# Eight experts on one core: samples in fixed slots, prompt tokens in 120, the gate applied as Y is evicted, Y scattered in a high and a low part

## The chip, the cores and the metric

The kernel runs on one core of one Trainium2 chip. The metric is the device time of that core in microseconds (us), as the median of several runs. The profile is of one execution on the same core.

## What is computed

One step of a two-layer trunk (SSD and RG-LRU mixers, a dense SwiGLU in layer 0, two of eight experts in layer 1) for 256 prompt tokens and 8 sample tokens, width 1024. The change touches the experts alone:

```python
def swiglu(x, wg, wu, wd):
    return (jax.nn.silu(x @ wg) * (x @ wu)) @ wd

def moe_swiglu(x, w_r, wg, wu, wd):
    logits = (x @ w_r).astype(jnp.float32)
    top_v, top_i = lax.top_k(logits, TOP_K)            # TOP_K = 2
    gates = jax.nn.softmax(top_v, axis=-1)
    dense_gate = jnp.sum(jax.nn.one_hot(top_i, N_EXPERTS, dtype=jnp.float32) * gates[..., None], axis=-2)
    out = jnp.zeros_like(x)
    for e in range(N_EXPERTS):                         # 8 experts, inner width 3584
        out = out + dense_gate[..., e:e + 1].astype(x.dtype) * swiglu(x, wg[e], wu[e], wd[e])
    return out
```

Everything is float32. After it comes a last RMSNorm of the prompt rows and the sample rows.

## The kernel before

The engines run programs of their own, written out in the order in which they issue, and meet by semaphores. The experts' part is a loop of **jobs**, one per expert (if an expert gets more tokens than it has slots, all eight are run again in a second and third pass, up to 24 jobs; `passes` decides it).

**Weights.** An expert's weights come as 42 units of 128x2048 floats (1 MB each), in the order of `STREAM`: step s = 0 to 6 takes two units of gate, two of up, and two of down for the step before (6 units in a full step). SP loads them into a ring of 6 slots (L631). ScalarE (ACT) rounds a unit to `w_hi` (fp32r), VectorE (DVE) subtracts it into `w_lo` (also fp32r); three slots of each. A product is three fp32r matmuls in TensorE (PE): `hi*hi`, `lo*hi`, `hi*lo` (`product`), so a unit is 12 matmuls of 128x512 and an expert 504. ACT may round unit p only when PE has used up unit p-3, and DVE follows ACT: this chain of PE, ACT, DVE and PE again (`split` on both engines) comes round once in three units.

**Tokens.** `sel_m` says which token lies in which of the 128 slots of the expert. `gather` turns it into the expert's input, XG transposed, by full fp32 matmuls: 8 blocks of 128 columns, for each the three token tiles (128, 128 and 8 rows). ACT and DVE evict it as `xg_hi` and `xg_lo`. It is made one job ahead: at the end of job j, between `transposes(6)` and `down(6)`, for job j+1. Right behind it three transposes bring the gated selection `sel_g` into S_BANK, which DVE copies to `sct`.

**Results.** Y of a job (two banks, 128 slots x 1024) is copied to `ysb` by ACT (`ysb`, 2 ACTIVATEs in the last iteration of its job loop). In the next job, after `down` of steps 0 to 5, `scatter(p)` makes one full fp32 matmul `sct` by `ysb` each, for token tile p//2 and column half p%2; two of the six have only the 8 sample rows. DVE adds the result to `acc` (`add_back`). After the last job six scatters follow through one bank, each waiting for the add before it; then ACT and DVE normalise the three tiles and POOL stores them.

In the profile a full fp32 matmul stands as two MATMUL records, an fp32r matmul and a transpose (`flip`, L806) as one; L802 is `mm`. L1211 is ACT's `f`, L1506 DVE's `tt`, L1503 its `stt`. `hntok`, `acc`, `ysb`, `sel_m`, `sel_g` and, before the change, `sct` all lie in `moe_arena` and bear its name.

## Time and profile before

| | us |
|---|---|
| median of 3 runs | 1937.28 |
| lowest, highest | 1935.87, 1945.31 |
| span of the profiled execution | 1943.8 |
| experts' products, first to last (850.15 to 1917.6) | 1067 |

The three runs are 1935.87, 1945.31 and 1937.28 us; of the profiled execution only its span is given, 1943.8 us from the first instruction to the last. PE is busy for 95% of that span, DVE for 71%, ACT for 55%, and the mean granted clock is 0.963 of full speed. A row of the timeline gives an instruction's start, its time, its operands and the idle time before it with what ended it. Successive matmuls overlap in it, so what one of them costs is the distance from its start to the next one's start, not its own time.

### The profile page before, as it was taken

What the parts mean: (1) busy time and instruction counts of PE and PEld (TensorE: products, weight loads), DVE (VectorE), ACT (ScalarE), POOL (GpSimd) and SP (SyncE); (2) the same over time, 40 slices, a digit from 0 to 9 for tenths busy, and PEclk for the clock granted to TensorE, in tenths of its full rate; (3) what the DMA queues carried; (4) which work ended last, traced back from release to release, by engine and by line L of the source; (5) the groups of instructions that cost most, each with busy time, mean ns of one, the idle gap of its engine ahead of it and who ended that gap; (6) DMA issues with size and microseconds to landing.
All of it is one profiled execution on the core that took longest, in us unless ns stands there. A gap on an engine that the chain in (4) does not pass through costs nothing.

```text
span 1943.8 us, 24842 instructions
## 1 busy us (share of the span) xinstructions
PE 1845.3 (95%) x9284; PEld 1513.6 (78%) x9284; DVE 1371.4 (71%) x1458; ACT 1075.4 (55%) x1101; POOL 167.2 (9%) x175
## 2 busy tenths in 40 slices
PE   7989889999999988889999999999999999999996
PEld 5867778999886677868778778787787787787873
DVE  4655865554465487458879788788788787887883
ACT  2236444443222654346667577676676775776772
POOL 2014530000100453000000000000000000000000
PEclk9999889999999988879999999999999999999997
DMA  8424434555643443339979899799799798997980
GB/s 246 136 89 150 140 112 145 181 151 168 193 130 100 136 135 121 119 136 365 351 285 360 296 346 358 271 369 360 277 365 352 279 365 284 358 355 284 364 321 24
DMA packets 257030, 465.48 MB, mean 239 GB/s; under 512 B 8492, under 2 KB 108196, under 8 KB 256928
## 3 DMA queue, kind: packets, MB, share of 16 engines
q1 hardware_dynamic: 249384, 441.84, 65.6%
q0 software_dynamic: 6384, 21.28, 3.7%
q10 hardware_dynamic: 1192, 1.44, 0.3%
q8 instruction: 43, 0.70, 0.2%
q14 instruction: 27, 0.22, 0.0%
HBM read 453.70 MB, written 11.15 MB: 239 GB/s over the span
## 4 chain that ended last, share of the span: by engine, by line
PE 86%; DVE 8%; ACT 3%; issue 2%; ACTq 0%; DMA 0%; POOL 0%; DVEq 0%; POOLq 0%
PE bank L802 83%; DVE arena L1503 3%; PE bank L806 2%; DVE arena L1506 1%; ACT w_hi L1211 1%; ACT arena L1211 1%; DVE w_lo L1506 1%; DVE fw_lo L1506 1%; DMA arena<-in_state_lru_conv 0%; DVE rs L1506 0%; DVE rs L1760 0%; ACTq L592 0%; ACT L1211 0%; ACT moe_arena L1211 0%; DVE rs L1535 0%
## 5 line engine op out<-in xcount | busy, mean ns | idle before, releaser
L1506 DVE TENSOR_TENSOR w_lo<-wring,w_hi 128x2048 fp32r<-128x2048 f32 x336 | 768.3, 2290 | 128.9 <-ACT w_hi L1211 127.1
L1211 ACT ACTIVATE w_hi<-wring 128x2048 fp32r<-128x2048 f32 x336 | 643.7, 1919 | 248.7 <-PE bank L802 248.5
L802 PE MATMUL bank<-w_hi,xg_hi 128*128 128x512 f32 x896 | 370.9, 414 | 3.0 <-DVE xg_lo L1506 1.6
L802 PE MATMUL bank<-w_lo,xg_hi 128*128 128x512 f32 x896 | 351.0, 392 | 0.0
L802 PE MATMUL bank<-w_hi,xg_lo 128*128 128x512 f32 x896 | 349.9, 390 | 0.0
L802 PE MATMUL bank<-hn,wring 128*128 128x264 f32 x1152 | 273.1, 398 | 6.1 <-DVE hn L1503 6.1
L802 PEld LDWEIGHTS bank<-hn,wring 128*128 128x128 f32 x1152 | 223.1, 196 | 50.8 <-issue 9.8
L802 PEld LDWEIGHTS bank<-w_hi,xg_hi 128*128 128x128 f32 x896 | 168.9, 189 | 55.6 <-issue 16.5
L802 PEld LDWEIGHTS bank<-w_hi,xg_lo 128*128 128x128 f32 x896 | 169.3, 189 | 39.9 <-issue 7.7
L802 PEld LDWEIGHTS bank<-w_lo,xg_hi 128*128 128x128 f32 x896 | 168.7, 188 | 36.9
L1506 DVE TENSOR_TENSOR fw_lo<-wring,fw_hi 128x2048 fp32r<-128x2048 f32 (+1 forms) x54 | 115.2, 2134 | 109.7 <-ACT fw_hi L1211 109.7
L802 PE MATMUL bank<-w_hi,at_hi 128*128 128x512 f32 x448 | 175.1, 391 | 0.0
L802 PE MATMUL bank<-w_hi,at_lo 128*128 128x512 f32 x448 | 174.4, 389 | 0.0
L802 PE MATMUL bank<-w_lo,at_hi 128*128 128x512 f32 x448 | 174.3, 389 | 0.0
L1211 ACT ACTIVATE arena<-bank 128x264 f32<-128x264 f32 (+3 forms) x100 | 43.1, 444 | 218.5 <-PE bank L802 207.6
L802 PE MATMUL bank<-moe_arena 128*128 128x128 f32 (+2 forms) x540 | 142.4, 387 | 11.4 <-DVE moe_arena L1863 6.2
L1211 ACT ACTIVATE fw_hi<-wring 128x2048 fp32r<-128x2048 f32 (+1 forms) x54 | 94.8, 1756 | 89.8 <-PE bank L802 89.8
L802 PEld LDWEIGHTS bank<-moe_arena 128*128 128x128 f32 (+1 forms) x540 | 79.1, 194 | 45.2 <-issue 17.0
L802 PEld LDWEIGHTS bank<-w_lo,at_hi 128*128 128x128 f32 x448 | 84.1, 188 | 17.6
L802 PEld LDWEIGHTS bank<-w_hi,at_hi 128*128 128x128 f32 x448 | 84.1, 188 | 17.4
L802 PEld LDWEIGHTS bank<-w_hi,at_lo 128*128 128x128 f32 x448 | 84.1, 188 | 17.2
L773 POOL DMA_DIRECT2D out<-moe_arena x2 | 1.1, 534 | 1117.5 <-DVE moe_arena L1503 1117.5
(215 smaller groups left out, 2329.9 us busy)
## 6 DMA issues: line engine op xcount, KB each, us to landing
wring<-in_moe_w_gate SPq DMA_DIRECT2D x112, 1024.0 KB, 5.2
wring<-in_moe_w_up SPq DMA_DIRECT2D x112, 1024.0 KB, 5.3
wring<-in_moe_w_down SPq DMA_DIRECT2D x112, 1024.0 KB, 5.1
wring<-in_w_in SPq DMA_DIRECT2D x36, 1024.0 KB, 5.2
wring<-in_w_out SPq DMA_DIRECT2D x16, 1024.0 KB, 5.1
wring<-in_ffn_w_gate SPq DMA_DIRECT2D x11, 1024.0 KB, 5.3
wring<-in_ffn_w_up SPq DMA_DIRECT2D x11, 1024.0 KB, 5.4
wring<-in_ffn_w_down SPq DMA_DIRECT2D x16, 704.0 KB, 4.6
```

The lines of the kernel that those rows point to most:

```text
L773: pool.dma_start(o[0][0, t * P:(t + 1) * P, :], outt[:, t, :]).then_inc(y_out, 16)
L802: return nc.tensor.matmul(out, lhsT, rhs, start=start, stop=stop)
L806: return nc.tensor.transpose(out, in_, ident[0:k, 0:k])
L1211: return nc.scalar.activation(out, in_, fn, **kw)
L1503: return V.scalar_tensor_tensor(out=out, in0=in0, scalar=scalar, in1=in1, op0=op0, op1=op1)
L1506: return V.tensor_tensor(out, in0, in1, op)
```

## The change

SLOTS becomes 120. Slots 120 to 127 of every expert hold the eight samples: they are written into `xg_hi` and `xg_lo` once, before the first job, and the gather fills the other 120 columns from two token tiles, not three. A sample that did not choose an expert has gate 0 there. Token tile 2 is now tokens 136 to 263, of which only rows 120 to 127 count.

The gate no longer sits in the scatter matrix. `slots_back(j)` in step 5 transposes `sel_m` of the job at hand (two transposes) and makes `gslot`, the gate of each slot, with three matmuls of one column; DVE copies both out and only then chooses for the next job (`choose`, so far in step 2's iteration). At the end of a job ACT evicts Y times `gslot` as `ysb_hi` (fp32r), and DVE (`results`) makes `ysb_lo` and adds the sample rows straight into `acc`. There are four scatters a job, each as two fp32r matmuls (`ysb_hi`, `ysb_lo`) with `sct` as the stationary side. After the last job the four scatters go to four banks. The output tiles are normalised in the order 2, 0, 1.

```diff
-SLOTS = P
-SCATTERS = 7
+SLOTS = P - NB
+S_FILLS = 5
...
+        TOK0 = (0, P, T - P)
+        ROWS = (slice(0, P), slice(0, P), slice(96, P))
...
+        TAIL_BANKS = (BA, BB, BN, Q0)
...
-                    ins = mm(out[0:n, t * NE:(t + 1) * NE], hn[:, k, t * P:t * P + n], w_router[:, k, :],
+                    ins = mm(out[:, t * NE:(t + 1) * NE], hn[:, k, TOK0[t]:TOK0[t] + P], w_router[:, k, :],
...
-            for t in range(4):
-                terms = [(ones, i) for i in range(min(t, 3))] + ([(before, t)] if t < 3 else [])
+            for t in range(3):
+                terms = [(ones, i) for i in range(t)] + ([(before, t)] if t < 2 else [])
...
-                        for t in range(3):
-                            n = P if t < 2 else NB
-                            ins = mm(out[:, q * P:(q + 1) * P], hntok[0:n, t, d0:d0 + P], sel_m[0:n, t, :],
-                                     start=t == 0, stop=t == 2)
+                        for t in range(2):
+                            ins = mm(out[:, q * P:(q + 1) * P], hntok[:, t, d0:d0 + P], sel_m[:, t, :],
+                                     start=t == 0, stop=t == 1)
...
-            def scatter(p, n, last_adds=0):
+            def scatter(out, p):
 
                 t, h = p // 2, p % 2
-                rows = P if t < 2 else NB
-                if last_adds:
-                    pe.wait_ge(acc_done, last_adds)
-                else:
-                    pe.wait_ge(evac[S_BANK], moe0[S_BANK] + n)
-                mm(bank[S_BANK][0:rows, :], sct[:, t, 0:rows], ysb[:, 512 * h:512 * h + 512]
-                   ).then_inc(full[S_BANK], 1)
+                for i, y in enumerate((ysb_hi, ysb_lo)):
+                    ins = mm(out[:, :], sct[:, t, :], y[:, 512 * h:512 * h + 512], start=i == 0, stop=i == 1)
+                return ins
+
+            def slots_back(j):
+
+                pe.wait_ge(evac[S_BANK], moe0[S_BANK] + S_FILLS * j + 4)
+                out = bank[S_BANK]
+                for t in range(2):
+                    flip(out[:, t * P:(t + 1) * P], sel_m[:, t, :])
+                for t in range(3):
+                    ins = mm(out[:, 2 * P:2 * P + 1], sel_m[:, t, :] if t < 2 else ident[:, :], cur[:, 2, t:t + 1],
+                             start=t == 0, stop=t == 2)
+                ins.then_inc(full[S_BANK], 1)
...
-                        pe.wait_ge(ysb_ready, 2 * j + 1)
+                        pe.wait_ge(y_free, j + 1)
                     if s > 0:
                         down(s - 1, j, STREAM.index(("d", s - 1, 0)), n - 1)
-                        scatter(s - 1, j * SCATTERS + s - 1)
+                    if 0 < s < 5:
+                        pe.wait_ge(evac[S_BANK], moe0[S_BANK] + S_FILLS * j + s - 1)
+                        scatter(bank[S_BANK], s - 1).then_inc(full[S_BANK], 1)
+                    if s == 5:
+                        slots_back(j)
...
-                pe.wait_ge(selg_ready, j + 1)
-                pe.wait_ge(evac[S_BANK], moe0[S_BANK] + j * SCATTERS + 6)
-                for t in range(3):
-                    n = P if t < 2 else NB
-                    ins = flip(bank[S_BANK][:, t * P:t * P + n], sel_g[0:n, t, :])
-                ins.then_inc(full[S_BANK], 1)
...
-            pe.wait_ge(ysb_ready, 2 * jobs + 1)
-            for p in range(6):
-                scatter(p, jobs * SCATTERS + p, last_adds=p)
+            pe.wait_ge(y_free, jobs + 1)
+            for p in range(4):
+                scatter(bank[TAIL_BANKS[p]], p).then_inc(tail_full, 1)
...
+            xs = hn[:, :, TP:T]
+            f(xg_hi.rearrange("p i (q s) -> p (i q) s", s=P)[:, :, SLOTS:P], xs).then_inc(xs_ready, 1)
...
+                        act.wait_ge(evac[S_BANK], moe0[S_BANK] + (j + 1) * S_FILLS)
                         for h in range(2):
-                            f(ysb[:, 512 * h:512 * h + 512], bank[Y_BANKS[h]][:, :]).then_inc(ysb_ready, 1)
+                            f(ysb_hi[:, 512 * h:512 * h + 512], bank[Y_BANKS[h]][:, :], scale=gslot[:, :]
+                              ).then_inc(ysb_ready, 1)
...
+                V.tensor_copy(gate_of[:, js, 0:2].rearrange("p e t -> p t e"), gates[:, 0:2, :])
+                if p == 0:
+                    V.tensor_copy(gate_of[:, js, 2:3].rearrange("p e t -> p t e"), gates[:, 2:3, :])
+                else:
+                    V.memset(gate_of[:, js, 2:3], 0.0)
+            V.memset(sel_m[:, :, :], 0.0)
+            V.memset(sct[:, :, :].bitcast(F32), 0.0).then_inc(sct_zero, 1)
...
-                for t in range(3):
-                    ins = V.tensor_scalar(sel_m[:, t, :], iota[:, :], cur[:, 0, t:t + 1], cur[:, 1, t:t + 1],
-                                          ALU.is_equal, ALU.mult)
+                for t in range(2):
+                    ins = V.tensor_scalar(sel_m[:, t, 0:SLOTS], iota[:, 0:SLOTS], cur[:, 0, t:t + 1],
+                                          cur[:, 1, t:t + 1], ALU.is_equal, ALU.mult)
                 ins.then_inc(selm_ready, 1)
 
-            def gated(j):
-                dve.wait_ge(selm_ready, j + 1)
-                for t in range(3):
-                    ins = V.tensor_scalar(sel_g[:, t, :], sel_m[:, t, :], cur[:, 2, t:t + 1], None, ALU.mult)
-                ins.then_inc(selg_ready, 1)
-
             choose(0)
-            gated(0)
             for p in range(1, SPLITS):
                 split(0, p)
...
-                evacd(tt(xg_lo[:, i], filled("gather", i)[:, :], xg_hi[:, i].bitcast(F32), ALU.subtract), "gather", i)
-
-            def add_back(p, n):
+                evacd(low_slots(i, filled("gather", i)), "gather", i)
+
+            def add_back(out, p):
                 t, h = p // 2, p % 2
-                rows = P if t < 2 else NB
-                dve.wait_ge(full[S_BANK], moe0[S_BANK] + n + 1)
-                v = acc[0:rows, t, 512 * h:512 * h + 512]
-                return tt(v, v, bank[S_BANK][0:rows, :], ALU.add)
+                v = acc[:, t, 512 * h:512 * h + 512]
+                return tt(v, v, out[:, :], ALU.add)
+
+            def results(j):
+
+                for h in range(2):
+                    dve.wait_ge(ysb_ready, 2 * j + h + 1)
+                    hs = slice(512 * h, 512 * h + 512)
+                    stt(ysb_lo[:, hs], bank[Y_BANKS[h]][:, :], gslot[:, :], ysb_hi[:, hs].bitcast(F32), ALU.mult,
+                        ALU.subtract)
+                    v = acc[ROWS[2], 2, hs]
+                    ins = stt(v, bank[Y_BANKS[h]][ROWS[2], :], gslot[ROWS[2], :], v, ALU.mult, ALU.add)
+                ins.then_inc(y_free, 1)
...
-                    if (mat, h) == ("d", 1) and s < STEPS - 1:
-                        add_back(s, j * SCATTERS + s).then_inc(evac[S_BANK], 1)
-                    if (mat, s, h) == ("d", 2, 1):
+                    if (mat, h) == ("d", 1) and s < 5:
+                        dve.wait_ge(full[S_BANK], moe0[S_BANK] + j * S_FILLS + s + 1)
+                        if s < 4:
+                            add_back(bank[S_BANK], s).then_inc(evac[S_BANK], 1)
+                    if (mat, s, h) == ("d", 4, 1):
+                        V.tensor_copy(gslot[:, :], bank[S_BANK][:, 2 * P:2 * P + 1])
+                        V.tensor_copy(sct[:, :, :], bank[S_BANK][:, 0:2 * P].rearrange("p (t n) -> p t n", t=2)
+                                      ).then_inc(evac[S_BANK], 1)
+                        dve.wait_ge(evac[S_BANK], moe0[S_BANK] + (j + 1) * S_FILLS)
                         choose(j + 1)
                     if (mat, s, h) == ("d", STEPS - 2, 1):
                         low_part(STEPS - 1, n + 1)
                         for i, b in enumerate(X_BANKS):
                             dve.wait_ge(xg_hi_ready, 2 * j + 2 + i + 1)
-                            tt(xg_lo[:, i], bank[b][:, :], xg_hi[:, i].bitcast(F32), ALU.subtract
-                               ).then_inc(evac[b], 1)
-                        dve.wait_ge(full[S_BANK], moe0[S_BANK] + j * SCATTERS + 7)
-                        V.tensor_copy(sct[:, 0:2, :], bank[S_BANK][:, 0:2 * P].rearrange("p (t n) -> p t n", t=2))
-                        V.tensor_copy(sct[:, 2, 0:NB], bank[S_BANK][:, 2 * P:2 * P + NB]).then_inc(evac[S_BANK], 1)
-                        gated(j + 1)
+                            low_slots(i, bank[b]).then_inc(evac[b], 1)
+                    if p == PER_JOB + SPLITS - 1:
+                        results(j)
...
+            V.memset(ysb_hi[:, :].bitcast(F32), 0.0)
+            V.memset(ysb_lo[:, :].bitcast(F32), 0.0).then_inc(y_free, 1)
...
-            for p in range(6):
-                add_back(p, jobs * SCATTERS + p).then_inc(acc_done, 1)
+            for p in range(4):
+                dve.wait_ge(tail_full, p + 1)
+                add_back(bank[TAIL_BANKS[p]], p).then_inc(acc_done, 1)
 
             dve.wait_ge(gfin_landed, 16)
-            for t in range(3):
-                n = P if t < 2 else NB
-                dve.wait_ge(act_step, 2 * t + 2)
-                link(V.reciprocal(ssum[0:n, t:t + 1], ssum[0:n, t:t + 1]))
-                stt(outt[0:n, t, :], acc[0:n, t, :], ssum[0:n, t:t + 1], gfin[0:n, :], ALU.mult, ALU.mult
-                    ).then_inc(y_ready, 1)
+            for i, t in enumerate((2, 0, 1)):
+                r = ROWS[t]
+                dve.wait_ge(act_step, 2 * i + 2)
+                link(V.reciprocal(ssum[r, t:t + 1], ssum[r, t:t + 1]))
+                stt(outt[r, t, :], acc[r, t, :], ssum[r, t:t + 1], gfin[r, :], ALU.mult, ALU.mult).then_inc(y_ready, 1)
```

PE around step 5 of a job, before: down(4), a scatter of the sample rows, and the next step's gate product.

```order
L802 MATMUL bank<-w_hi,at_hi 128x512
L802 MATMUL bank<-w_hi,at_lo 128x512
L802 MATMUL bank<-w_lo,at_hi 128x512
L802 MATMUL bank<-moe_arena 8x512
L1106 REGISTER_ALU
L1108 REGISTER_ALU
L802 MATMUL bank<-w_hi,xg_hi 128x512
```

The same place now (L810 is `mm`, L814 is `flip`):

```order
L810 MATMUL bank<-w_lo,at_hi 128x512
L1152 REGISTER_ALU
L814 MATMUL bank<-ident,moe_arena 128x128 x2
L810 MATMUL bank<-moe_arena 128x1 x2
L810 MATMUL bank<-moe_arena,ident 128x1
L1113 REGISTER_ALU
L1115 REGISTER_ALU
L810 MATMUL bank<-w_hi,xg_hi 128x512
```

The scatter is gone there, and `slots_back` has come in.

PE at the end of a job, before, between down(5) and down(6):

```order
L802 MATMUL bank<-moe_arena 8x512
L1116 REGISTER_ALU
L806 MATMUL bank<-ident,moe_arena 128x128 x4
L1164 REGISTER_ALU
L802 MATMUL bank<-moe_arena 128x128 x24
L1173 REGISTER_ALU
L806 MATMUL bank<-ident,moe_arena 128x128 x2
L806 MATMUL bank<-ident,moe_arena 128x8
```

And now:

```order
L810 MATMUL bank<-w_lo,at_hi 128x512
L1123 REGISTER_ALU
L814 MATMUL bank<-ident,moe_arena 128x128 x4
L1182 REGISTER_ALU
L810 MATMUL bank<-moe_arena 128x128 x16
L1130 REGISTER_ALU
L1133 REGISTER_ALU
L810 MATMUL bank<-w_hi,at_hi 128x512
```

The scatter before the transposes, 8 of the 24 gather matmuls and the three transposes behind them are gone.

DVE at the end of a job, before, from the evictions of the gathered input to the first three units of the next job:

```order
L1506 TENSOR_TENSOR xg_lo<-bank,xg_hi 128x512
L1917 REGISTER_ALU
L1918 COPY moe_arena<-bank 128x256
L1919 COPY moe_arena<-bank 128x8
L1870 TENSOR_SCALAR moe_arena<-moe_arena 128x128 x3
L1798 REGISTER_ALU
L1506 TENSOR_TENSOR w_lo<-wring,w_hi 128x2048
L1798 REGISTER_ALU
L1506 TENSOR_TENSOR w_lo<-wring,w_hi 128x2048
L1798 REGISTER_ALU
L1506 TENSOR_TENSOR w_lo<-wring,w_hi 128x2048
```

And now:

```order
L1523 TENSOR_TENSOR xg_lo<-bank,xg_hi 128x4x120
L1815 REGISTER_ALU
L1523 TENSOR_TENSOR w_lo<-wring,w_hi 128x2048
L1815 REGISTER_ALU
L1523 TENSOR_TENSOR w_lo<-wring,w_hi 128x2048
L1907 REGISTER_ALU
L1520 SCALAR_TENSOR_TENSOR ysb_lo<-bank,moe_arena,ysb_hi 128x512
L1520 SCALAR_TENSOR_TENSOR moe_arena<-bank,moe_arena 32x512
...
L1815 REGISTER_ALU
L1523 TENSOR_TENSOR w_lo<-wring,w_hi 128x2048
```

The small copies ahead of unit 0 are gone; `results` (four instructions, two of them left out above) stands between unit 1 and unit 2.

## Rows read from the trace of the kernel before

**Rows 1.** The page: busy time of each engine and share of the span.

```profile
PE 1845.3 (95%) x9284; PEld 1513.6 (78%) x9284; DVE 1371.4 (71%) x1458; ACT 1075.4 (55%) x1101; POOL 167.2 (9%) x175
```

**Rows 2.** Busy time by stretch: PE, PEld, DVE, ACT, POOL, clock, DMA share, GB/s.

```profile
1110.00:1245.00 135.00, 134.81 (x607) 106.85 (x606) 111.02 (x76) 92.02 (x62) 0.00 (x0) 1.00 0.92 326
```

**Rows 3.** Waits of PE from 1000 to 1800 us: total, times, longest.

```profile
PE bank L802 <- DVE w_lo L1506: 1.1, 5, 0.2
```

**Rows 4.** Timeline of PE, a 128-row scatter among products: start, us, instruction.

```profile
1280.51 0.39 PE L802 MATMUL bank<-w_lo,at_hi 128*128 128x512 f32 x1
1280.74 1.02 PE L802 MATMUL bank<-moe_arena 128*128 128x512 f32 x2
...
1281.82 0.39 PE L802 MATMUL bank<-w_hi,xg_lo 128*128 128x512 f32 x1
```

**Rows 5.** Timeline of PE, an 8-row scatter among products.

```profile
1218.09 0.39 PE L802 MATMUL bank<-w_lo,at_hi 128*128 128x512 f32 x1
...
1219.70 0.39 PE L802 MATMUL bank<-w_hi,xg_lo 128*128 128x512 f32 x1
...
1224.71 0.39 PE L802 MATMUL bank<-w_lo,xg_hi 128*128 128x512 f32 x1
```

**Rows 6.** Timeline of PE, gather and transposes at the end of a job.

```profile
1237.82 8.41 PE L802 MATMUL bank<-moe_arena 128*128 128x128 f32 x48
1246.16 0.59 PE L806 MATMUL bank<-ident,moe_arena 128*128 128x128 f32 x3
...
1247.02 0.39 PE L802 MATMUL bank<-w_hi,at_lo 128*128 128x512 f32 x1
```

**Rows 7.** Timeline of PEld (weight loads), matmuls of 8 columns in `rank`.

```profile
826.43 0.75 PEld L802 LDWEIGHTS bank<-moe_arena,ones 128*128 128x128 f32 x6
```

**Rows 8.** Timelines at a job's end: ACT's eviction of Y, DVE's splits, PE.

```profile
1252.46 1.09 ACT L1211 ACTIVATE moe_arena<-bank 128x512 f32<-128x512 f32 x2 [0.75 <-PE bank L802]
1253.43 1.92 ACT L1211 ACTIVATE w_hi<-wring 128x2048 fp32r<-128x2048 f32 x1
...
1251.74 2.29 DVE L1506 TENSOR_TENSOR w_lo<-wring,w_hi 128x2048 fp32r<-128x2048 f32 x1 [0.74 <-ACT w_hi L1211]
1255.38 2.29 DVE L1506 TENSOR_TENSOR w_lo<-wring,w_hi 128x2048 fp32r<-128x2048 f32 x1 [1.35 <-ACT w_hi L1211]
...
1260.95 0.50 PE L802 MATMUL bank<-w_hi,xg_hi 128*128 128x512 f32 x1 [0.22 <-DVE w_lo L1506]
```

**Rows 9.** The router's logits: timeline of PE, then its count in a stretch.

```profile
810.74 7.45 PE L802 MATMUL bank<-w_router,hn 128*128 128x8 f32 x48 [5.81 <-issue]
...
817.50:818.00 0.50, 0.50 (x16) 0.50 0.00 0
```

**Rows 10.** Router to first expert: timelines of PE and DVE, a stretch as rows 2.

```profile
833.50 15.03 PE L802 MATMUL bank<-moe_arena 128*128 128x128 f32 x48 [6.23 <-DVE moe_arena L1863]
...
830.69 0.91 DVE L1852 MEMSET moe_arena<- 128x1024 f32 x1 [0.15 <-issue]
...
850.00:856.00 6.00, 5.85 (x14) 4.59 (x15) 0.00 (x0) 0.24 (x1) 0.00 (x0) 0.50 0.00 0
```

**Rows 11.** The end: four steps of the chain of waits, then ACT's timeline.

```profile
1917.85 1.09 ACT moe_arena L1211 x2
...
1928.78 0.70 DVE moe_arena L1506
...
1936.25 1.29 DVE moe_arena L1503
...
1939.22 0.49 POOL out L775
...
1923.80 1.06 ACT L1211 ACTIVATE moe_arena<-moe_arena 128x1024 f32<-128x1024 f32 x1 [4.86 <-DVE moe_arena L1506]
...
1926.26 0.29 ACT L1211 ACTIVATE moe_arena<-moe_arena,eps 128x1 f32<-128x1 f32 x1
```

**Rows 12.** Busy time by stretch, columns as in rows 2, where the ring refills.

```profile
864.00:879.00 15.00, 15.00 (x69) 12.18 (x68) 13.61 (x8) 11.44 (x9) 0.00 (x0) 1.00 1.03 384
```

More of the change, by code:

```diff
@@ L413, in trunk @@
         cur = carve(3, 3)
-        sel_m = carve(3, P)
-        sel_g = carve(3, P)
-        sct = carve(3, P)
+        sel_m = carve(2, P)
+        gslot = carve(1)
         m1 = carve(3)
         gsum = carve(3)
-        outt = hntok
         gfin = carve(D)
```

79 lines of the change are left out of this document (44 added, 35 removed).

## The prediction

> **What bounds the kernel now.** I read the page first: PE is busy for 95% of the span, DVE for 71%, ACT for 55% [rows 1]. Then the busy time by stretch, for one expert out of the loop: PE is busy in all but 0.2 of 135 us, at full clock, DVE in 111, ACT in 92, and the weight stream brings 326 GB/s [rows 2]. Then PE's waits: from 1000 to 1800 us it stood still for 1.1 us in all, for DVE's `w_lo` [rows 3]. So in the experts PE's own instructions set the time, and whatever PE no longer does is won, as long as the weight splits and the stream keep up. Since matmuls overlap, I price each by the distance between starts. An fp32r product costs 0.228 us (22 distances in 1219.70 to 1224.71) [rows 5]; an expert's 42 units of 12 products make 115 us. The eight jobs take 1067 us from first to last product (table of times), 133 each, so some 18 us go to scatters, gather and transposes. The change works on these.
>
> **Scatters, per job.** From the product before a 128-row scatter to the second product behind it are 1.31 us, of which two are product distances: 0.86 us for the scatter [rows 4]. With 8 rows it is 1.61 - 0.46 = 1.15 us [rows 5]; fewer rows made it no cheaper. Before: 4 x 0.86 + 2 x 1.15 = 5.7 us. After: 4 x 2 fp32r matmuls of the shape of the products, 8 x 0.228 = 1.8 us. No row shows `sct` by `ysb_hi`, but its shape and type are those of rows 5; dearer than 0.35 each (a start and a stop in one bank) I would not expect. Gain 3.9 us, lower end 2.9.
>
> **Gather, per job.** 48 records in 8.34 us are 0.174 each [rows 6]. A third of them goes: 2.8 us. The evictions of 480 instead of 512 columns change nothing that counts.
>
> **`slots_back` for the three transposes, per job.** The transposes took 1246.16 to 1247.02 less one product, 0.63 us [rows 6]. Now there are two (0.42) and three fp32 matmuls of one column, six records. The nearest rows are `rank`'s with 8 columns, 0.125 a record [rows 7]: 0.75. Below it lies 0.04, the narrow router records [rows 9], above it the gather's 0.174. I take 1.15, net +0.5 us a job; ends 0.0 and +0.8.
>
> Together 3.9 + 2.8 - 0.5 = 6.2 us a job, eight jobs, the last one too: **-49.6 us**.
>
> **The new wait at the end of a job.** ACT may round unit 2 of the next job only when PE is through with down(6), and evicts Y first: at 1252.46, then unit 2 at 1253.43; DVE splits it from 1255.38 to 1257.67 [rows 8]. PE needs it 2 x 12 products after down(6), at 1257.7. It is just in time, and unit 3 is already 0.2 us late at 1260.95 [rows 8]. Now `results` stands on DVE between units 1 and 2: four instructions that wait for ACT's eviction. Behind them wait DVE's splits of units 2 and 3, and PE for them. DVE ends unit 1 at 1254.0 on that scale (1251.74 + 2.29). Since it no longer has the small copies to do and PE starts down(6) 0.5 us sooner, I reckon from the start S of down(6) (1246.68, where the gap behind the transposes of rows 6 ends): unit 1 done at S+7.3; `results` four times 0.6 (a 128x512 add takes 0.70 and overlaps by 0.1 [rows 11]) to S+9.7; unit 2 until S+12.0. PE needs it at S+11.05: 0.95 us late. Unit 3 was late before, by 0.5 us from start to start (12 products after 1257.7 would be 1260.45), and is now in time because PE comes later. Net **+0.45 us**, seven times: **+3.2**. Ends: 0 (if the four overlap more) and +1.5 (if each takes 0.85 and unit 3 is late too).
>
> **Other moves on DVE.** `choose` moves to step 4's iteration, where it takes the place of an add (0.6), with a copy and a cast of some 0.5. The copies and `sel_g` behind the gather and two 8-row adds are gone. DVE's sum stays near 111 us of now 127. The splits have about 0.8 us to spare a round of three units: PE frees a slot, ACT starts 0.4 us later, takes 1.92, DVE 2.29 [rows 8], against 3 x 2.72 us of PE. I cost it at nothing; the scatters that shrink were no part of that slack, they only lengthened it.
>
> **Head.** Router to first expert: token tile 2 is now 128 wide in the logits. Of 48 records the last 16 were narrow, at 0.04, the others 0.21 ((817.5 - 810.74) / 32) [rows 9]: +2.7 us. Eight transposes of `hntok` go, at 0.17 (0.52 / 3 [rows 6]): -1.4. On DVE the 0.91 us memset moves out of the way [rows 10] and small ones come and go. The first gather ran at half clock, 15.03 us [rows 10]; a third is 5.0. Sum **-4.6**, ends -2 and -7. The first products then run at half clock, 14 records in 6 us [rows 10], and the gain in starting sooner may shorten or lengthen this by 1.5 us.
>
> **Tail.** From ACT's eviction at 1917.85 to the last store's issue at 1939.22 are 21.4 us: six scatters in turn, each behind the add before [rows 11]. Now: eviction 0.6, `results` until 3.4, four pairs at half clock (0.43 a record) end at 7.1, adds (0.70) run beside. ACT's first norm starts at 5.2 behind the first add and takes 2.75 (1923.80 to 1926.55, with its table load), two more at 1.45: 10.9; DVE's last multiply 1.45 more: 12.3 [rows 11]. Saved 9.0, less 0.7 since the last store is now a 128-row tile: **-8.3**, ends -6 and -10.
>
> **Sum.** -49.6 + 3.2 - 4.6 - 8.3 = -59.3 us: the profiled span of 1943.8 becomes 1884.5. The profiled execution lies 6.5 us above the median of the runs, 1937.28; the same difference taken from that median gives **1878 us**.
>
> **A rule against it: the weight stream.** The stream brought 384 GB/s over 15 us when the ring refilled [rows 12] and has to bring 44.04 MB in 127 us, 347 on average, and 6.29 MB in 17.3 us within a step of 17.3 us (72 products, transposes, one scatter), 364. So the rows leave room. The Trainium skill, in DMA: Bandwidth & Descriptors, section Where 436 GB/s comes from, has transfers from HBM to SBUF bound at about 358 GB/s per core. By that a step's six loads take 17.6 us, more than PE's 17.3; but over a whole expert it would be 123 us, below the 127 of PE, and the ring's six slots even it out, so the sum would be the same. The trace goes above that figure, for 15 us at least.
>
> **Rivals.**
> 1. *The splits become the bound at the job's end.* `results` costs more than 0.6 an instruction, or its delay runs on through units 3 to 5. For it: unit 3 is late already [rows 8]. Against it: each later unit wins back 0.4 us on DVE. At 2.5 us a job: 7 x 2 more, 1892. Chance 0.10.
> 2. *The clock falls at the job's border.* PE idled 6.2 us before the first gather, and that gather and the first products ran at half clock [rows 10]; a wait of nearly 1 us now comes seven times. Against it: it is far shorter, and the waits of 0.2 us so far left the clock at 1.00 [rows 2, 8]. At half clock 14 records take 6 us instead of 3.2 [rows 10]: 7 x 2.8 = 20 more, 1898. Chance 0.06.
> 3. *The stream holds at what it shows for a whole expert, 326 GB/s* [rows 2]. Then a job stays at 133 us and only head and tail are won: 1924. Against it [rows 12]. Chance 0.03.
> 4. *Slower: a second pass.* If one expert gets over 120 prompt tokens (so far: over 128 tokens with the samples), `passes` becomes 24: sixteen more jobs of 127 us, 3910 us. The mean is 256 x 2 / 8 = 64. The reference's router on its own drawn inputs gives the fullest expert 96 prompt tokens, so it decides only for other inputs. Chance 0.01.
> 5. *The fp32r scatter is no cheaper than the fp32 one* (a pair at 0.86): 4 x 0.4 x 8 = 13 less won, 1891. Chance 0.05.
>
> **How the numbers follow.** My case has 0.75. Its open ends: scatters +8, `slots_back` -4 to +3, the wait -3 to +7, head and tail -4 to +5; not all at once, -13 to +15. With rivals 1, 2 and 5 inside, the range is 1864 to 1899. A measurement of this kernel tells about 0.5% (10 us) from no change; faster by more than that holds in all cases but rival 4 and something unseen: faster 0.96, same 0.02, slower 0.02.
>
> **What would show it.** In the profile after: two records of `ysb_hi` and `ysb_lo` at 0.23 us start to start; a gather of 32 records in 5.6 us; a job of 127 us from gather to gather; PE waiting for `w_lo` once a job by 0.7 to 1.0 us at unit 2, right behind four SCALAR_TENSOR_TENSOR on DVE; the clock at 1.00 throughout the loop; 340 to 350 GB/s. I am wrong if the job takes over 129 us, or if PE's waits in the loop exceed 2 us a job.

## The result, and the profile after

The changed kernel takes 1889.62 us (median of 4 runs, 1887.01 to 1891.59), the kernel before 1937.01 beside it: a ratio of 0.974, 95% interval 0.972 to 0.976. Its profiled execution spans 1887.7 us, 56.1 less than before. That is more than the 47.4 us between the medians, because the profiled execution before was a long one: its span of 1943.8 us exceeds the whole time of the other three runs before (1935.87, 1936.75 and 1937.28 us). The page, busy time of each engine:

```profile
PE 1782.1 (94%) x9128; PEld 1490.4 (79%) x9128; DVE 1377.5 (73%) x1438; ACT 1076.2 (57%) x1102; POOL 167.1 (9%) x175
```

PE still sets the time; it is busy for 63 us less than in [rows 1]. One whole job, from gather to gather, as in [rows 2] (us, then PE, PEld, DVE, ACT, POOL, clock, DMA share, GB/s):

```profile
1103.00:1231.60 128.60, 127.32 (x581) 103.21 (x580) 111.95 (x74) 92.20 (x63) 0.00 (x0) 1.00 0.96 342
```

DVE and ACT do about the same work as before in 4.6 us less, the clock is full, and the stream brings 342 GB/s; before it was 326 in the window of [rows 2], and 331 from gather to gather. PE, which was busy for all but 0.2 us, now stands still for 1.3. From start of gather to start of gather the job takes 128.56 us (1088.21, 1216.77), before it took 133.20 (1104.63, 1237.82). The span's loss splits into four parts (the jobs are eight times 4.64, and the first products what is left between them and the head):

| us | forecast | measured |
|---|---|---|
| start to first product of the experts | -4.6 | -8.8 |
| first products at full instead of half clock | 0 | -2.9 |
| eight jobs | -46.4 | -37.1 |
| tail | -8.3 | -7.2 |
| sum | -59.3 | -56.0 |

The timeline of PE, a scatter among products (start, us, instruction), against [rows 4, 5]:

```profile
1127.38 0.39 PE L810 MATMUL bank<-ysb_hi,sct 128*128 128x512 f32 x1
1127.61 0.39 PE L810 MATMUL bank<-ysb_lo,sct 128*128 128x512 f32 x1
1127.84 0.40 PE L810 MATMUL bank<-w_hi,xg_hi 128*128 128x512 f32 x1
```

The pair costs 0.46 us from start to start, where one fp32 matmul cost 0.86. `slots_back`, and the gather against [rows 6]:

```profile
1198.20 0.38 PE L814 MATMUL bank<-ident,moe_arena 128*128 128x128 f32 x2
1198.42 0.50 PE L810 MATMUL bank<-moe_arena 128*128 128x1 f32 x4
1198.78 0.36 PE L810 MATMUL bank<-moe_arena,ident 128*128 128x1 f32 x2
1199.01 0.48 PE L810 MATMUL bank<-w_hi,xg_hi 128*128 128x512 f32 x1
...
1216.77 3.74 PE L810 MATMUL bank<-moe_arena 128*128 128x128 f32 x32
1220.26 0.48 PE L810 MATMUL bank<-w_hi,at_hi 128*128 128x512 f32 x1
```

32 records go by in 3.49 us, 0.109 each; before they were 0.174 each. `slots_back` takes 0.81 us. The place of the new wait, DVE and PE:

```profile
1225.34 2.29 DVE L1523 TENSOR_TENSOR w_lo<-wring,w_hi 128x2048 fp32r<-128x2048 f32 x1
1227.55 0.75 DVE L1520 SCALAR_TENSOR_TENSOR ysb_lo<-bank,moe_arena,ysb_hi 128x512 fp32r<-128x512 f32 x1
1228.31 0.76 DVE L1520 SCALAR_TENSOR_TENSOR moe_arena<-bank,moe_arena 32x512 f32<-32x512 f32 x1
...
1230.64 2.29 DVE L1523 TENSOR_TENSOR w_lo<-wring,w_hi 128x2048 fp32r<-128x2048 f32 x1
...
1231.31 0.40 PE L810 MATMUL bank<-w_lo,xg_hi 128*128 128x512 f32 x1
1232.98 0.50 PE L810 MATMUL bank<-w_hi,xg_hi 128*128 128x512 f32 x1 [1.28 <-DVE w_lo L1523]
```

Each of the four `results` instructions takes 0.77 us, unit 2 is split by 1232.93, and PE gets it 1.67 us after the product before it, 1.44 more than a product distance. PE's waits from 1000 to 1800 us (total, times, longest), against [rows 3]:

```profile
PE bank L810 <- DVE w_lo L1523: 7.7, 6, 1.3
```

And this, which the forecast has no step for: two products of one stretch, 40 product distances apart, nothing but products between; first now, then such a stretch of before.

```profile
1117.11 0.40 PE L810 MATMUL bank<-w_hi,xg_lo 128*128 128x512 f32 x1
...
1126.45 0.40 PE L810 MATMUL bank<-w_lo,at_hi 128*128 128x512 f32 x1
```

```profile
1137.57 0.40 PE L802 MATMUL bank<-w_hi,xg_lo 128*128 128x512 f32 x1
...
1146.65 0.39 PE L802 MATMUL bank<-w_lo,at_hi 128*128 128x512 f32 x1
```

The 9.34 us by 40 are 0.2335 us a product, at full clock and with no wait; 22 of before took 0.228 each [rows 5], and these 40 of before took 9.08, 0.227. Times 504 products this is worth 3 us a job. Most of the experiments are about it.

Head: the first gather and the first product of the experts, against [rows 10].

```profile
834.22 5.62 PE L810 MATMUL bank<-moe_arena 128*128 128x128 f32 x32 [6.01 <-DVE moe_arena L1884]
841.38 0.49 PE L810 MATMUL bank<-w_hi,xg_hi 128*128 128x512 f32 x1 [1.54 <-DVE xg_lo L1523]
841.71 0.40 PE L810 MATMUL bank<-w_hi,xg_lo 128*128 128x512 f32 x1
```

Busy time by stretch during this gather (columns as above):

```profile
836.00:838.00 2.00, 2.00 (x12) 2.00 (x11) 2.00 (x2) 0.00 (x0) 0.00 (x0) 0.50 0.40 31
838.00:840.00 2.00, 1.84 (x16) 1.65 (x15) 1.02 (x2) 0.69 (x2) 0.00 (x0) 1.00 0.95 358
```

The clock rose from 0.50 to 1.00 about two thirds through the gather, so that the products behind it are 0.23 to 0.33 us apart and not 0.43. Before, it rose only at 856 us, 22 us after the gather's start. Tail: ACT's eviction, the first scatter matmul, the four adds, the last store, against [rows 11].

```profile
1868.94 1.26 ACT L1223 ACTIVATE ysb_hi<-bank,moe_arena 128x512 fp32r<-128x512 f32 x2 [5.08 <-PE bank L810]
...
1872.78 0.80 PE L810 MATMUL bank<-ysb_hi,sct 128*128 128x512 f32 x1 [3.92 <-DVE moe_arena L1520]
...
1874.33 2.70 DVE L1523 TENSOR_TENSOR moe_arena<-moe_arena,bank 128x512 f32<-128x512 f32 x4 [1.61 <-PE bank L810]
...
1882.58 0.54 POOL L781 DMA_DIRECT2D out<-moe_arena  x1 [0.85 <-DVE moe_arena L1520]
```

From eviction to the last store's issue are 13.6 us, before 21.4. The forecast had 12.3 and 0.7 more behind the issue. Of the 1.3 us between them 0.4 lies ahead of the first scatter (3.84 us after the eviction began, not 3.4), which is `results` again, 0.5 between it and the first add (1.55 us, not 1.1), and 0.4 between ACT's last norm step and the store's issue.

The tail before is not the same in every execution. Its second scatter, in the chain of waits of the kernel before and then of a kernel of experiment 3 (offsets 256; 1024), which differs from it only in places in SBUF:

```profile
1920.96 2.09 PE bank L802 x2
```

```profile
1919.30 1.14 PE bank L806 x2
```

In the first the clock had fallen to 0.50 at 1920.9 us, in the second it stayed at 1.00 until 1929.1. From the last product's start to the end of the span the first takes 26.5 us and the second 21.9. The kernels of experiments 2, 3 and 5 leave this tail's program as it was, and they show the same two lengths: 21.9 us four times and 26.4 or 26.5 twice. The changed kernel's is 19.3. So 4.5 of the 7.2 us won in the tail hang on the execution that was profiled before.

### The profile page after: what moved, and what is told of

It is laid out like the page before. It is cut to its first block, busy times and chain, and to the rows that moved or that the text cites. A ratio compares the mean times of both kernels' runs of the same rounds, so it can differ in the third digit from the quotient of the medians.

```text
span 1887.7 us, 24534 instructions
## 1 busy us (share of the span) xinstructions
PE 1782.1 (94%) x9128; PEld 1490.4 (79%) x9128; DVE 1377.5 (73%) x1438; ACT 1076.2 (57%) x1102; POOL 167.1 (9%) x175
## 3 DMA queue, kind: packets, MB, share of 16 engines
q10 hardware_dynamic: 1192, 1.44, 0.3%
## 4 chain that ended last, share of the span: by engine, by line
PE 85%; DVE 9%; ACT 3%; issue 2%; ACTq 1%; DMA 0%; POOL 0%; DVEq 0%; POOLq 0%
PE bank L810 83%; DVE arena L1520 3%; PE bank L814 2%; ACT arena L1223 1%; DVE arena L1523 1%; DVE w_lo L1523 1%; DVE moe_arena L1520 1%; DVE fw_lo L1523 1%; DMA arena<-in_state_lru_conv 0%; ACT L1223 0%; DVE rs L1523 0%; DVE rs L1777 0%; ACTq L600 0%; ACT ysb_hi L1223 0%; DVE rs L1552 0%
## 5 line engine op out<-in xcount | busy, mean ns | idle before, releaser
L810 PE MATMUL bank<-w_hi,xg_hi 128*128 128x512 f32 x896 | 359.0, 401 | 10.6 <-DVE w_lo L1523 9.0
L810 PE MATMUL bank<-w_lo,xg_hi 128*128 128x512 f32 x896 | 354.5, 396 | 0.0
L810 PE MATMUL bank<-w_hi,xg_lo 128*128 128x512 f32 x896 | 354.4, 396 | 0.0
L810 PE MATMUL bank<-hn,wring 128*128 128x264 f32 x1152 | 272.5, 397 | 6.2 <-DVE hn L1520 6.1
L810 PEld LDWEIGHTS bank<-hn,wring 128*128 128x128 f32 x1152 | 222.7, 196 | 50.6 <-issue 9.8
L810 PEld LDWEIGHTS bank<-w_hi,xg_hi 128*128 128x128 f32 x896 | 168.4, 188 | 52.6 <-DVE w_lo L1523 12.6
L810 PEld LDWEIGHTS bank<-w_lo,xg_hi 128*128 128x128 f32 x896 | 168.2, 188 | 40.3
L810 PEld LDWEIGHTS bank<-w_hi,xg_lo 128*128 128x128 f32 x896 | 168.4, 188 | 38.2
L810 PE MATMUL bank<-w_hi,at_lo 128*128 128x512 f32 x448 | 177.7, 397 | 0.0
L810 PE MATMUL bank<-w_hi,at_hi 128*128 128x512 f32 x448 | 177.1, 395 | 0.0
L810 PE MATMUL bank<-w_lo,at_hi 128*128 128x512 f32 x448 | 176.6, 394 | 0.0
L810 PEld LDWEIGHTS bank<-w_hi,at_hi 128*128 128x128 f32 x448 | 84.1, 188 | 20.7
L810 PEld LDWEIGHTS bank<-w_lo,at_hi 128*128 128x128 f32 x448 | 84.1, 188 | 20.0
L810 PEld LDWEIGHTS bank<-w_hi,at_lo 128*128 128x128 f32 x448 | 84.1, 188 | 19.8
L810 PE MATMUL bank<-hn_hi,fw_hi 128*128 128x264 f32 x352 | 88.9, 288 | 4.4 <-ACT hn_hi L1223 4.4
L810 PE MATMUL bank<-hn_hi,fw_lo 128*128 128x264 f32 x352 | 88.8, 287 | 0.0
```

Source lines behind the costliest of these rows:

```text
L810: return nc.tensor.matmul(out, lhsT, rhs, start=start, stop=stop)
```

## The experiments

**What can make the same product dearer?** The change moves buffers. `sct` now stands ahead of `w_hi`, and paddings went in, so the operands of a product lie elsewhere in SBUF. (In `product`, `xg` or `at` is the stationary operand, 128x128, and w the moving one, 128x512.) In bytes of a partition, modulo 256: before, `w_hi`, `w_lo`, `xg_hi`, `xg_lo`, `at_hi` and `at_lo` all are at 128; now `w_hi` and `w_lo` are at 0 and the other four at 160. Theory A: it is where the stationary operand itself lies. Theory G, formed when A fell: it is the distance between the stationary operand (xg, at) and the moving one (w). The expectations of experiment 4 have these two names the other way round. The rival of both is that the order of the changed program, or its fuller stream, slows PE. (Where an expectation names a further theory by a letter, it says there what that theory holds.)

**1. The stationary operands back to where they were modulo 256.** `xg` and `at` at 128, w left at 0.

```diff
-        sb("to_hn", [P, 552])
+        sb("to_hn", [P, 544])
...
         xg_hi, xg_lo = (sb(n, [P, 2, 4 * P], F32R) for n in ("xg_hi", "xg_lo"))
+        sb("to_ysb", [P, 32])
```

> The changed kernel with one difference: the stationary operands at_hi, at_lo, xg_hi, xg_lo start 32 bytes lower in SBUF, on a multiple of 128 bytes as they did before the change (in the changed kernel they start 32 bytes past one); ysb_hi and ysb_lo move up by 96 bytes. Same instructions, same order. Theory A, placement: the distance between products, 0.2332 us in the changed kernel against 0.2267 before, comes from where the stationary operands lie. Then it goes back to 0.2267, 504 products a job win 3.3 us, 8 jobs 26 us: about 1863 us, with PE's wait for w_lo at unit 2 somewhat longer (1.6 to 1.8 us). Theory B, company: the distance grew because DVE and the weight stream have less time per product now. Then it stays at 0.233 and the time at 1889.

Measured: 1885.16 us (1880.93 to 1886.12), ratio to before 0.9729 (0.9713 to 0.9745). Theory A wanted 1863 us; this is 4 us under the changed kernel. Forty product distances took 9.34 us (1115.47 to 1124.81), as in the changed kernel, and a job 128.27 us, 0.3 less. A falls: the stationary operand's own place is not enough.

**2. The kernel before, with its stationary operands shifted by 32 bytes.**

```diff
         w_hi, w_lo = (sb(n, [P, SPLITS, UNIT], F32R) for n in ("w_hi", "w_lo"))
+        sb("shift", [P, 8])
```

> The kernel before with one difference: a gap of 32 bytes ahead of xg_hi, so that xg_hi, xg_lo, at_hi, at_lo start 32 bytes past a multiple of 128. Theory A, placement: the products come at 0.2332 instead of 0.2267 us, 4032 of them cost 26 us more: about 1963 us. Theory B, company: nothing changes, 1937 us.

Measured: 1956.82 us (1956.7 to 1962.45), ratio 1.0116 (1.0099 to 1.0133), 20 us slower by nothing but a gap, where 26 were expected. Forty product distances of this kernel:

```profile
1138.13 0.39 PE L803 MATMUL bank<-w_hi,xg_lo 128*128 128x512 f32 x1
...
1147.46 0.40 PE L803 MATMUL bank<-w_lo,at_hi 128*128 128x512 f32 x1
```

Here 40 take 9.33 us, 0.233 each: the dear product stands in the old program, with the old stream. So neither the new order nor the stream makes it. The job takes 135.65 us, 2.45 more than before.

**3. All six buffers shifted by 32 bytes, and other distances.** In the kernel before. First, the gap ahead of `w_hi`, so that everything moves together:

```diff
+        sb("shift", [P, 8])
         w_hi, w_lo = (sb(n, [P, SPLITS, UNIT], F32R) for n in ("w_hi", "w_lo"))
```

> The kernel before, all of w_hi, w_lo, xg_hi, xg_lo, at_hi, at_lo 32 bytes further. Relative places are as before, absolute ones are not a multiple of 64. Theory G, relative place: 0.2267, 1937 us. Theory H, absolute place: 0.233, 1957 us, as where the stationary operands alone were shifted.

Then gaps in front of single buffers. With `xg_hi` 0, `xg_lo` 128 and `at` 2048 bytes past a multiple of 4096 from w:

```diff
+        sb("to_xg_lo", [P, 32])
         xg_lo = sb("xg_lo", [P, 2, 4 * P], F32R)
+        sb("to_at_hi", [P, 480])
```

> The kernel before, only the places of the stationary operands differ. Measured from the moving operand w_hi modulo 4096 bytes (where all four lay at 0 before): xg_hi 0, xg_lo 128, at_hi 2048, at_lo 2048. Read from the trace: the distance between products of each kind. Theory G, relative place: a product takes 0.2267 us only where the stationary operand lies at 0 from the moving one (modulo some power of two up to 4096). Then the products next to xg_lo go to 0.233 and those with at_hi and at_lo tell whether the power is above 2048. Theory H, absolute place of w: the changed kernel is slower because w_hi starts at a multiple of 256 there and not here; then all stay at 0.2267 here, and only shifts that are no multiple of 64 cost. Time 1937 to 1960 us.

With `xg` 256 and `at` 1024 bytes past it (gaps of 64 and 192 floats):

> As the run before, with xg_hi and xg_lo at 256 and at_hi and at_lo at 1024 from w_hi modulo 4096. Theory G: 0.233 where 256 or 1024 is not a multiple of the period, 0.2267 where it is. Theory H: 0.2267 for all. Time 1937 to 1960 us.

With `xg_hi` 64, `xg_lo` 192 and `at` 256 (gaps of 16, 32 and 16 floats):

> The kernel before with xg_hi 64 bytes and xg_lo 192 bytes past a multiple of 256 from w_hi and w_lo, and at_hi and at_lo a multiple of 256 from them as before. So far 0, 256, 1024 and 2048 gave 0.2267 us between products, and 32, 128 and 160 gave 0.233. Theory G1 (a multiple of 256 bytes is wanted): both 64 and 192 are slow, the 336 gate and up products of a job at 0.233, those of down at 0.2267: 336 x 8 x 0.0065 = 17 us more than the kernel before, 1954 us. Theory G2 (the period is 64 and 128 was slow for another reason): all fast, 1937. Between them: one of the two slow, 1942 to 1950, and then the products beside xg_lo and those beside xg_hi alone differ.

Measured, each beside before on its own chip, with the time of 40 product distances of a stretch like those above, a job from gather to gather, and the mean distance, from 1000 to 1750 us, behind each kind of product (the three kernels in the middle were run once each):

| | us | before | 40 distances | job | hi by `xg_hi` | hi by `xg_lo` | lo by `xg_hi` | hi by `at_hi` |
|---|---|---|---|---|---|---|---|---|
| before | | | 9.08 | 133.20 | 0.229 | 0.227 | 0.229 | 0.227 |
| only xg, at by 32 | 1956.8 | 1936.6 | 9.33 | 135.65 | 0.233 | 0.233 | 0.233 | 0.233 |
| all by 32 | 1940.0 | 1939.3 | 9.09 | 133.33 | 0.228 | 0.228 | 0.229 | 0.227 |
| 0, 128; 2048 | 1946.5 | 1939.3 | 9.15 | 134.00 | 0.232 | 0.234 | 0.228 | 0.227 |
| 256; 1024 | 1939.6 | 1939.3 | 9.09 | 133.20 | 0.228 | 0.227 | 0.229 | 0.227 |
| 64, 192; 256 | 1952.0 | 1944.7 | 9.21 | 134.38 | 0.229 | 0.235 | 0.231 | 0.229 |

The jobs say more than the times: the tail told of above (26.4 or 26.5 us against 21.9) adds 4.5 us to an execution, as it did in the one of 1946.5. Shifting all six costs 0.1 us a job at most: what counts is the relation. The offsets 0, 256, 1024 and 2048 bytes are cheap, 32 and 128 dear. (The 128-column tiles inside `xg` and `at` themselves lie 512 bytes apart, those of w 2048, so whole multiples of 512 could not differ.) With `xg_lo` at 128, two distances are dear, the one from the product before it to it and the one from it to the next; the third of each round is not. The last kernel came in between: 1.0036 of before (1.002 to 1.0051), +7 us, or 1.2 us a job, where 17 (2.2 a job) were expected if both 64 and 192 were dear and none if neither was. Here the distance behind the product with `xg_lo` (at 192) is dear at 0.235, the one behind its successor slightly (0.231), and the one ahead of it, behind `xg_hi` at 64, is as before. So "a multiple of 256 or the full price" is too simple; how dear each offset between is stays open.

**4. The changed kernel with the relation restored.** Two ways. Both buffers at 128 modulo 256, as in the kernel before:

```diff
         sct = sb("sct", [P, 2, P], F32R)
+        sb("to_w", [P, 32])
...
-        sb("to_hn", [P, 552])
+        sb("to_hn", [P, 512])
...
+        sb("to_ysb", [P, 32])
```

> The changed kernel with its split and input buffers put back in the relation that they had before the change: w_hi and w_lo start 128 bytes further in each partition, and xg and at 32 bytes earlier, so that the distance between a product's stationary operand (w) and its moving one (xg, at) is again a multiple of 256 bytes. Nothing else differs. Theory G (the relation of the two operands' places sets the distance between products: a multiple of 256 bytes gives 0.2267 us, 32, 128 or 160 give 0.2332): products at 0.2267, 504 x 0.0065 = 3.3 us a job less, less up to 0.5 that PE waits longer at unit 2 because DVE does not get faster: 2.8 to 3.3 x 8 = 22 to 26 us, so 1864 to 1867 us beside 1889.6 for the changed kernel, ratio to the kernel before 0.963. PE's wait at unit 2 grows from 1.4 to about 1.7. Rival 1 (the order of the changed program or the stream sets the distance): products stay at 0.233, 1885 to 1890 us. Rival 2 (products get shorter but DVE and ACT are now the bound of the whole loop): products at 0.2267, waits of 3 to 4 us a job spread over the units, 1880 to 1890 us.

And with `xg` and `at` left at their 160, w brought there too (`to_w` of 40 floats, `to_hn` of 512, and no `to_ysb`):

> The changed kernel with xg and at exactly where it has them (160 bytes past a multiple of 256) and w_hi and w_lo moved by 160 bytes to match. Theory G, the relation alone counts: as the kernel with both at 128: 1864 to 1867 us, products at 0.2267. Rival: it is the moving operand's own place that counts, too: products at 0.233, or between, 1875 to 1890 us.

Measured: 1867.57 us (1862.9 to 1870.35), ratio 0.964 (0.962 to 0.9661), and 1866.52 us (1863.45 to 1869.24), ratio 0.9627 (0.9602 to 0.9653), where Theory G had 1864 to 1867. Of the first kernel, 40 product distances:

```profile
1123.99 0.39 PE L812 MATMUL bank<-w_hi,xg_lo 128*128 128x512 f32 x1
...
1133.07 0.39 PE L812 MATMUL bank<-w_lo,at_hi 128*128 128x512 f32 x1
```

A job's busy time, as above:

```profile
1113.00:1238.60 125.60, 124.08 (x581) 103.00 (x580) 111.70 (x74) 91.96 (x63) 0.00 (x0) 1.00 0.96 350
```

PE's waits from 1000 to 1800 us:

```profile
PE bank L812 <- DVE w_lo L1525: 9.2, 6, 1.5
```

The products take 9.08 us for 40, 0.227 each. The job is 125.79 us long, 2.77 less than the changed kernel's. By the waits (9.2 us in six instead of 7.7) 0.25 us a job came back as a longer wait for DVE. Both versions beat both kernels: 22 and 23 us under the changed one, 70 under the one before, for some unused bytes of SBUF.

**5. The gather's third tile with 128 rows, in the kernel before.** Theory C: matmuls of only 8 rows are what made the gather's records 0.174 each; the record of a whole tile costs 0.11. The rival: all records cost 0.174, and the changed kernel's are cheaper for another reason. The edit does the same number of matmuls, the third tile's with zeros in 120 rows.

```diff
-                            n = P if t < 2 else NB
-                            ins = mm(out[:, q * P:(q + 1) * P], hntok[0:n, t, d0:d0 + P], sel_m[0:n, t, :],
+                            ins = mm(out[:, q * P:(q + 1) * P], hntok[:, t, d0:d0 + P], sel_m[:, t, :],
...
+            link(V.memset(hntok[:, 2, :], 0.0))
```

> The kernel before, but the gather's third token tile has 128 rows, 120 of them zero, instead of 8 (one more memset in the head; the result is the same). Theory C, short tiles are dear: in the changed kernel a gather record costs 0.109 us where it cost 0.174 before, because none has only 8 rows. Then the 48 records here take about 5.2 us instead of 8.34 in a steady job, and the first gather 5.5 to 8 instead of 15: -3.1 x 8 - 8 = about -33 us, 1904 us. Rival D: a record's price falls with their number or with what the banks hold, not with the rows: 8.3 us stay, 1937 to 1938 us.

Measured: 1905.71 us (1901.44 to 1907.49), ratio 0.9837 (0.982 to 0.9853). More arithmetic, and 31 us less. Its gather inside the loop:

```profile
1221.41 5.52 PE L802 MATMUL bank<-moe_arena 128*128 128x128 f32 x48
1226.77 0.54 PE L806 MATMUL bank<-ident,moe_arena 128*128 128x128 f32 x3
```

48 records in 5.36 us, 0.112 each, where [rows 6] has the same 48 in 8.34. C holds. Record by record, the two of an 8-row matmul, the one ahead of them and the one behind stand 0.20 to 0.21 us apart, all others 0.11. Whether it is the 8 rows that cost, or the passing from 128 rows to 8 and back, no run tells apart. A job takes 130.18 us, 3.0 less; the first gather took 8.17 us, not 15.03, with the clock at 1.00 from 838 us on, 5.4 us after its start and not 22. So the early clock of the changed kernel, too, comes with the short matmuls' going. A large part of the change's gain is had by this edit alone.

**6. `results` spread over the next job's units.** Theory: PE's wait at unit 2 is the 3.1 us of `results` on DVE at one place; spread, the wait goes. Rival: DVE and ACT have no slack at the job's border, and the wait moves. First, the four instructions behind units 6 to 9 of the next job:

```diff
+                    if SPLITS <= p - 3 < SPLITS + 4:
+                        result(j, p - 3 - SPLITS)
...
-                    if p == PER_JOB + SPLITS - 1:
-                        results(j)
```

> The changed kernel, but the four instructions that make ysb_lo and add the sample rows stand in the next job, one each behind the low parts of units 6 to 9, instead of together between units 1 and 2 (for the first job they work on zeros). Theory E: PE's wait at unit 2, 1.44 us from start to start, is due to them. Then the wait falls to what it was before, 0.3 to 0.5 us in all at units 2 and 3, and seven jobs win about 1 us each: 1882 us. Rival F: unit 2 is late because of ACT (eviction of Y, table load), the wait stays above 1 us and the time at 1889 us.

Measured: 1927.84 us (1924.52 to 1933.59), 38 us slower than the changed kernel, ratio to before 0.9953 (0.9937 to 0.9968). PE at down(0), which needs Y's banks:

```profile
1138.13 0.49 PE L810 MATMUL bank<-w_hi,at_hi 128*128 128x512 f32 x1 [3.50 <-DVE moe_arena L1520]
...
1139.60 0.63 PE L810 MATMUL bank<-w_lo,at_hi 128*128 128x512 f32 x1
1140.03 0.63 PE L810 MATMUL bank<-w_hi,at_hi 128*128 128x512 f32 x1
```

PE's waits from 1000 to 1800 us:

```profile
PE bank L810 <- DVE moe_arena L1520: 21.0, 6, 3.5
PE bank L814 <- DVE moe_arena L1523: 1.9, 5, 0.4
PE bank L810 <- DVE w_lo L1523: 0.8, 5, 0.2
```

The wait for `w_lo` went as meant (0.8 in all), but down(0) came 3.5 us before Y was free, six times; and behind it products were 0.43 us apart, half clock, for 3.4 us (1139.17 to 1142.57). Over all eight jobs the clock fell seven times, five times for 3.4 us and twice for 6.8; behind the wait at 1806 us it did not. This is the size of wait at which rival 2 of the prediction comes true. Then earlier, behind units 4 to 7 of the next job, on top of the layout of experiment 1:

```diff
+                    if 4 <= p < 8:
+                        result(j, p - 4)
```

> The changed kernel with its stationary operands on a multiple of 128 bytes and with the four instructions that make ysb_lo and add the sample rows spread over the next job, one behind the low part of each of units 4 to 7 (two units earlier than in e4_results_spread, where PE waited 3.5 us a job for the last of them ahead of down(0) and then ran at half clock for 4 us). Theory E: now neither unit 2 nor down(0) waits; PE's waits fall from 1.4 us a job to below 0.6 and seven jobs win 6 us against 1885: 1879 us. Rival: the pieces make the low parts of units 4 to 8 late, each by a few tenths, and nothing is won: 1885 us or more.

Measured: 1887.23 us (1886.9 to 1892.42), against 1885.16 without the spreading: no gain, and a job of 129.07 us against 128.27. PE's waits from 1000 to 1800 us:

```profile
PE bank L815 <- DVE moe_arena L1524: 7.7, 6, 1.5
PE bank L811 <- DVE w_lo L1524: 0.8, 5, 0.2
```

The same 7.7 us in six waits, now ahead of the transposes, which need DVE's product of gate and up. So between units 1 and 2 and behind units 4 to 7 the work costs the same wait: of DVE's 3.1 us of extra work PE waited for some 1.3. Placed behind units 6 to 9, PE's waits for DVE's other work were small (1.9 and 0.8 us in all), and it was Y's banks, held too long, that cost the time. A version that spreads the work that late and still frees the banks early was not run.

## Why the forecast came out as it did

1889.6 lies within 1864 to 1899, 12 us above the forecast of 1878, and the mechanism is in the main as told: scatters and gather give the gain, and PE waits for `w_lo` at unit 2. The clock at 1.00 in the loop and 340 to 350 GB/s (342) came as written; the job, at 128.56 us, did not come down to 127 and lies just under the 129 that would have meant wrong.

The 12 us are of two kinds. Only 3 of them are in the table of the span above (56.0 won, 59.3 forecast). The other 8 come from the step "the same difference taken from that median": it took off 6.5 us for an execution that lay above the median, but left the whole gain, read from that execution, as it was. Its tail was 4.5 us longer than in four of the six other traces with the same tail, as shown above, and the six scatters of that long tail are what the forecast of -8.3 was worked out from. That the runs at the median had the shorter tail is inferred, since none of them was traced, and the rest of the 8 is not located.

And that only 3 us are missing in the span is in part luck: two misses cancel. Per job, in us:

| | forecast | measured | |
|---|---|---|---|
| scatters | -3.9 | -3.9 | pair at 0.46 |
| gather and three transposes | -3.4 | -5.4 | 32 records at 0.109 |
| `slots_back` | +1.15 | +0.9 | |
| wait at unit 2 | +0.45 | +1.0 | 1.44, less 0.47 that was there |
| distance between products | 0 | +2.8 | SBUF places |
| sum | -5.7 | -4.6 | 133.20 to 128.56 |

- **Scatters**: right, and rival 5 (no cheaper than fp32) fell with the rows of the pair.
- **Gather**: the mis-sized step is "48 records in 8.34 us are 0.174 each. A third of them goes". It took a mean over unlike records as the price of each. The third that goes is the dear one, and it made its neighbours dear. The rows had given a hint [rows 4, 5]: a scatter with 8 rows cost 1.15 us, more than the 0.86 of one with 128. (There it is the output that has 8 rows, in the gather the contraction, so it is a hint and no more.) The prediction noted "fewer rows made it no cheaper" and did not carry it to the gather. Its open end should then have reached to a gain in which the short third is dearer than the rest. Experiment 5 alone gives 3.0 us of the job.
- **The wait**: place, cause and the absence of a wait at unit 3 were right, its size was not. `results` cost 0.77 an instruction instead of 0.6; the price came from an add of PSUM and SBUF [rows 11], with no row for a SCALAR_TENSOR_TENSOR that reads PSUM (the one of L1503 there, 1.29 us for 1024 columns, reads SBUF). Four times 0.17 are the 0.7 us by which unit 2 came late: at S+12.67 (S is 1220.26) where the step had S+12.0. PE, at dearer products, asked for it 0.2 later than reckoned. Rival 1 (2.5 us a job) did not come. Of the prediction's other moves on DVE, the slack of 0.8 us is right only against the two units of PE between the freed slot and its next use (2 x 2.72 us), not against the three that it names.
- **Products**: the failed step is that "An fp32r product costs 0.228 us" was carried over as a constant of the kernel; it measured 0.2334 in the mean, from 1000 to 1750 us. No step asked what the diff's paddings and the new buffers do to the operands' places. That is 2.8 x 8 = 22 us, what experiment 4 gets back (22 and 23 us). Without it the change comes out at 1867, 11 below the forecast.
- **Head**: logits as forecast (10.38 us against 7.45, +2.9). But the gather took 5.62 us, then the first product came at 841.38, 7.16 after its start instead of 16.65: -9.5 where -5.0 was reckoned, again for the price of the short records, and because the clock rose inside the gather. From logits to gather, 1.6 us were lost and not 0.4. The 0.9 won ahead of the logits (809.84 against 810.74) is not shown to be a gain: in the six kernels that differ from before only in places or in the gather's third tile the logits began anywhere from 805.2 to 809.7. The early clock also gave the first products 2.9 us.
- **Tail**: -7.2 against -8.3, of which `results` is 0.4; against a tail before at full clock it would be -2.7.
- **The stream** (rival 3) did not bind: 342 GB/s over a job. In experiment 4 it was 350, at a DMA share of 0.96. The Trainium skill, DMA: Bandwidth & Descriptors, section Where 436 GB/s comes from, has HBM to SBUF bound at some 358 GB/s; no whole job here goes above it, though 15 us of the kernel before did, with 384 [rows 12]. An estimate by that rule is that a job of 44.04 MB takes 123 us at least; no run here tried a shorter one.
- **The clock** (rival 2) stayed at 1.00 in the loop: 1.3 us of idle time did not lower it, 3.5 us did, seven times of eight (experiment 6).

What stays open: why the distance between the operands' places matters, and by which function of it; the one job border of experiment 2 at which the clock was 0.57 for some 4 us with no wait of PE (that job took 137.19 us and is left out of the 135.65); and why the tail before keeps its clock in some executions and loses it in others.

## What to carry to other kernels

A mean over a group of unlike instructions is not the price of one: if a change takes out the odd ones, look at what they cost apart from the others, and do not take an fp32 matmul of few rows to be cheaper than a full one: here it was dearer. When the profiled execution lies off the median of the runs, see first which part of it is long: a gain read from that part is not there in the other executions. When a diff moves buffers, compare the distance between a hot matmul's two operands in SBUF before and after, and measure the distance between successive starts: it costs a few bytes of padding to restore. Work added to an engine that is nearly late can give a wait at the next place, too, when it is spread; moving it further from its producer also holds the banks that it reads.

## What the runs showed of the hardware

- The same fp32r product, 128x128 by 128x512, at full clock: 0.227 us from start to start where the buffers of w and of the input start a multiple of 256 bytes apart, 0.233 where they start 32, 128 or 160 bytes past one; 2.5 to 3.0 us in a job of 504 (experiments 2 and 4). With `xg_hi` at 64 and `xg_lo` at 192 the mean distances were 0.229, 0.231 and 0.235, by the pair of neighbours (experiment 3).
- An fp32 matmul of 128 columns with 128 rows in its contraction: 0.11 us a record; with 8 rows, its two records and the one on either side 0.20 to 0.21 (experiment 5).
- A SCALAR_TENSOR_TENSOR that reads PSUM costs 0.77 us from start to start with 128x512 and with 32x512: fewer rows saved nothing here either.
- After PE stood still for 3.5 us, its products ran at half clock for 3.4 us (twice 6.8 us, once not at all); after 1.3 us they did not. After 6 us of idle time ahead of the first gather the clock came back 4 us into it in the changed kernel and 5 us with the third tile filled, but 22 us into it with the 8-row matmuls.
- Six scatters in turn, each behind the add before it: 1.14 us each where the clock stayed at 1.00 and 2.09 where it fell, for the same instructions; 4.5 us of the whole in some executions and not in others.
